# Latent attention of a hybrid encoder: full-precision products of scores and values turned into three rounded products each

## The chip, the cores and the metric

One core of a Trainium2 chip runs the whole program. The metric is the device time of one execution in microseconds (us), the median over several executions. The engines are TensorE (PE in the profile; its weight loads are PEld), VectorE (DVE), ScalarE (ACT), GpSimd (POOL) and SyncE (SP, which issues most transfers).

## What is computed

The reference is one encoder layer over 1024 tokens of width 1024: a layer norm, one input projection, three groups of heads side by side (RWKV-7 time mixing, 2-D neighbourhood attention, latent attention), an output projection, a norm, a SwiGLU FFN and a norm. The change concerns the third group only:

```python
def mla_attention(p, q_norm_g, w_q_b, kv_norm_g, w_kv_b, cos, sin):
    B, T, _ = p.shape
    c_q, c_kv, k_pe = jnp.split(p, [MLA_Q_RANK, MLA_Q_RANK + MLA_KV_RANK], -1)
    q = (rms_norm(c_q, q_norm_g) @ w_q_b).reshape(B, T, MLA_HEADS, MLA_NOPE_DIM + MLA_ROPE_DIM)
    kv = (rms_norm(c_kv, kv_norm_g) @ w_kv_b).reshape(B, T, MLA_HEADS, MLA_NOPE_DIM + MLA_V_DIM)
    q_nope, q_pe = jnp.split(q, [MLA_NOPE_DIM], -1)
    k_nope, v = jnp.split(kv, [MLA_NOPE_DIM], -1)
    q_pe = apply_rope(q_pe, cos[:, None, :], sin[:, None, :])
    k_pe = apply_rope(k_pe, cos, sin)
    q = jnp.concatenate([q_nope, q_pe], -1)
...
    scale = (MLA_NOPE_DIM + MLA_ROPE_DIM) ** -0.5
...
        s = jnp.einsum('bqhd,bkhd->bhqk', q_blk, k).astype(jnp.float32) * scale
        prob = jax.nn.softmax(s, axis=-1)
        return jnp.einsum('bhqk,bkhd->bqhd', prob.astype(v.dtype), v)
```

There are 8 such heads; queries and keys have 64 + 32 columns each, values 64. `k` is `k_nope` with the one `k_pe` beside it in every head. All data are float32.

## The kernel before

Each engine has its own program, written out by hand in the order in which it runs, and the programs meet only through semaphores (`wait_ge`, `then_inc`). Nothing reorders them, so an instruction that waits holds up all that stands behind it on its engine. On-chip memory is one large tile, `arena`, cut by hand into regions; most names in the profile are therefore `arena`. PSUM has eight banks of 512 columns.

The latent attention stands between the neighbourhood attention and the RWKV scan. Its heads are numbered (i, b): pair i from 0 to 3, and b 0 or 1, which also picks the buffers. Eight heads run one after another, and inside a head `kt` counts eight steps of 128 keys. On TensorE a step is:

- `scores` (L1609): keys of the step against all 1024 queries, in two halves of 512 columns, into banks 0 and 1 or 2 and 3 in turn. Rows 0 to 63 hold the plain part, 64 to 95 the rotary part, row 96 of the keys is 1 and row 96 of the queries is minus the row's maximum, so that the maximum is subtracted in the product.
- `values` (L1619): 64 columns of values and 64 columns of ones against the exponentials of the step, summed over the steps in banks 6 and 7. Rows 0 to 63 become the output, rows 64 to 127 the sums of the exponentials.
- `guard` (L1591): rounded scores of the next head, 128 queries against all keys, in banks 4 and 5. VectorE takes their maximum (`head_max`, L1152), which is the maximum that the next head will subtract. The guards were already in the rounded form (`q_round`, `k_round`, type fp32r).

`scores` and `values` take float32 operands; each such product of 512 columns is two matmul instructions in the profile. A rounded product (fp32r) is one.

Between steps ScalarE takes the exponential of a step's scores out of PSUM (`head_exps`, L827) into a ring of three buffers. At the end of a head TensorE turns the maxima into a row (`turn_max`, L1597), which goes by ScalarE (`copy_max`, L798) and a transfer on the SP queue (`head_loads`, L491) into row 96 of the queries; TensorE projects queries, keys and values of the head after next (`head_project`, L1568 and L1572; `head_values`, L1578), ScalarE copies them out (`head_copies`, L784 to L794) and VectorE applies the rotary turn (`head_rope`, L1126 to L1131) and copies the output out (`head_out`, L1158).

Three more things share these engines here. In pair 0, VectorE makes two running sums in each head (`sums`: eight scans L1137, a factor L1139, a sum L1141), and ScalarE makes exponentials of them (`decays`, L808) before steps 2 and 6. While it does so, GpSimd multiplies tiles of 128 x 1024 for the scan (L609 to L620: six instructions for each of four q; the last two wait for `decays`). In pairs 1 to 3, VectorE divides the outputs of the pair before in four pieces (`divide`, L1167 and L1170) while head b = 0 runs.

## Time and profile before

| | |
|---|---|
| median of 3 runs | 1875.41 us (1871.94 to 1876.02) |
| the profiled execution, own time | 1872.56 us |
| its span, first to last instruction | 1870.7 us |
| busy: PE, DVE, ACT, POOL | 92%, 44%, 29%, 19% of the span |
| mean granted TensorE clock | 0.972 |
| latent attention, from the first scores of head (0,0) to the end of head (3,1) | 409.85 to 727.3 us |

The busy shares are means over stages with different limits; what a stage is worth is read from its own rows. A granted clock of 1.00 is TensorE at 2.4 GHz, 0.50 is 1.2 GHz. The chain that ended last is followed back from the end of the program: what stands in it is what the time is made of.

### The profile page before, as it was taken

The numbers are of one execution on the slowest core, as the hardware profiler recorded it, in microseconds if no ns is written. First come the engines' busy times: TensorE is split into PE (matmuls) and PEld (weight loads), VectorE is DVE, ScalarE is ACT, GpSimd is POOL, SyncE is SP. The second block draws the span as 40 slices with busy tenths as digits, with TensorE's granted clock in tenths as the row PEclk, the third lists the DMA queues.
The fourth block names the chain that finished last, engine by engine and source line by source line (L and its number), as shares of the span: only waits on it lengthen the run. The fifth ranks groups of instructions, "written<-read, shape, count | busy, mean of one in ns | idle before, by whom it ended". The sixth has DMA issues, their size and how long they took to land.

```text
span 1870.7 us, 22729 instructions
## 1 busy us (share of the span) xinstructions
PE 1722.4 (92%) x8988; PEld 1224.1 (65%) x8988; DVE 824.8 (44%) x1161; ACT 534.1 (29%) x994; POOL 348.7 (19%) x359
## 2 busy tenths in 40 slices
PE   2999988889999987899999997999999999999995
PEld 2888745644444443577774455888888888888884
DVE  7324329765545444666655365111111111233546
ACT  3111167734333332444441012112111111232321
POOL 0700001128200000877860044000000000000000
PEclk8999999989999998899999998999999999999998
DMA  5311000000000000000005003111111111244233
GB/s 194 117 63 45 12 30 1 1 16 5 4 4 4 4 1 14 2 3 2 2 2 213 12 12 135 46 45 45 54 58 45 45 45 45 81 155 132 93 101 112
DMA packets 24278, 93.50 MB, mean 50 GB/s; under 512 B 2752, under 2 KB 5120, under 8 KB 23568
## 3 DMA queue, kind: packets, MB, share of 16 engines
q1 hardware_dynamic: 23744, 87.27, 13.7%
q0 software_dynamic: 464, 5.28, 0.7%
q8 instruction: 46, 0.75, 0.2%
q14 instruction: 24, 0.20, 0.0%
HBM read 79.92 MB, written 12.58 MB: 49 GB/s over the span
## 4 chain that ended last, share of the span: by engine, by line
PE 87%; DVE 8%; ACT 3%; issue 1%; DMA 1%; SPq 0%; POOL 0%; DVEq 0%; ACTq 0%; POOLq 0%
PE psum L1860 26%; PE psum L1886 12%; PE psum L1468 9%; PE psum L1609 6%; PE psum L1811 6%; PE psum L1619 5%; PE psum L1486 2%; PE psum L1568 2%; PE psum L1550 2%; PE psum L1591 2%; PE psum L1531 1%; PE psum L1493 1%; PE psum L1710 1%; DVE stats L1152 1%; PE psum L1706 1%
## 5 line engine op out<-in xcount | busy, mean ns | idle before, releaser
L1860 PE MATMUL psum<-h_hi,w_hi 128*128 128x512 f32 x704 | 275.2, 391 | 11.7 <-DVE h_lo L1348 11.7
L1860 PE MATMUL psum<-h_lo,w_hi 128*128 128x512 f32 x704 | 274.6, 390 | 0.0
L1860 PE MATMUL psum<-h_hi,w_lo 128*128 128x512 f32 x704 | 274.6, 390 | 0.0
L1381 DVE TENSOR_TENSOR arena<-psum,arena 128x1024 f32 (+1 forms) x22 | 26.9, 1225 | 391.7 <-ACT arena L928 391.7
L1860 PEld LDWEIGHTS psum<-h_hi,w_hi 128*128 128x128 f32 x704 | 132.7, 188 | 39.9 <-DVE h_lo L1348 12.0
L1860 PEld LDWEIGHTS psum<-h_lo,w_hi 128*128 128x128 f32 x704 | 132.6, 188 | 27.7 <-issue 0.2
L1860 PEld LDWEIGHTS psum<-h_hi,w_lo 128*128 128x128 f32 x704 | 132.6, 188 | 27.6
L1152 DVE TENSOR_REDUCE stats<-psum 128x1 f32<-128x1024 f32 x64 | 78.0, 1224 | 122.8 <-PE psum L1591 122.8
L1886 PE MATMUL psum<-wd_hi,act_hi 128*128 128x512 f32 x336 | 130.7, 389 | 0.0
L1886 PE MATMUL psum<-wd_lo,act_hi 128*128 128x512 f32 x336 | 130.7, 389 | 0.0
L1886 PE MATMUL psum<-wd_hi,act_lo 128*128 128x512 f32 x336 | 130.7, 389 | 0.0
L631 POOL TENSOR_TENSOR arena<-arena,consts 128x512 f32<-128x512 f32 x64 | 80.9, 1285 | 265.4 <-ACT arena L864 264.8
L1609 PE MATMUL psum<-arena 97*128 97x512 f32 x256 | 121.6, 602 | 3.2 <-DMA arena<-arena 2.2
L1619 PE MATMUL psum<-arena 128*128 128x512 f32 x256 | 120.3, 592 | 0.0
L1811 PE MATMUL psum<-arena 128*128 128x512 f32 x256 | 111.0, 593 | 1.9 <-DMA arena<-in_w_out 1.9
L1394 DVE TENSOR_TENSOR wd_lo<-arena,wd_hi 128x1024 fp32r<-128x1024 f32 x44 | 53.9, 1225 | 129.7 <-ACT wd_hi L942 129.7
L1468 PE MATMUL psum<-h_hi,w_in_hi 128*128 128x512 f32 x240 | 95.3, 397 | 11.1 <-DVEq L1013 11.1
L827 ACT ACTIVATE arena<-psum 128x1024 f32<-128x1024 f32 x64 | 65.4, 1022 | 133.5 <-PE psum L1609 133.5
L928 ACT ACTIVATE arena<-psum 128x1024 f32 (+1 forms) x22 | 22.6, 1027 | 273.9 <-PE psum L1860 273.9
L1468 PE MATMUL psum<-h_hi,w_in_lo 128*128 128x512 f32 x240 | 95.2, 397 | 0.0
L1468 PE MATMUL psum<-h_lo,w_in_hi 128*128 128x512 f32 x240 | 94.7, 395 | 0.0
L1811 PEld LDWEIGHTS psum<-arena 128*128 128x128 f32 x256 | 48.3, 190 | 63.7 <-issue 59.3
(263 smaller groups left out, 2851.6 us busy)
## 6 DMA issues: line engine op xcount, KB each, us to landing
arena<-in_w_down SPq DMA_DIRECT2D x44, 512.0 KB, 3.6
arena<-in_w_gate SPq DMA_DIRECT2D x22, 512.0 KB, 3.6
arena<-in_w_up SPq DMA_DIRECT2D x22, 512.0 KB, 4.6
arena<-in_w_in SPq DMA_DIRECT2D x15, 512.0 KB, 3.5
arena<-in_x SPq DMA_DIRECT2D x8, 512.0 KB, 9.7
resid_spill<-arena POOLq DMA_DIRECT2D x1, 4096.0 KB, 12.9
arena<-in_w_out SPq DMA_DIRECT2D x8, 512.0 KB, 6.6
arena<-resid_spill SPq DMA_DIRECT2D x1, 4096.0 KB, 20.0
```

What stands on the lines that cost most here:

```text
L631: pool.tensor_tensor(Lev[d][m % 2], Araw[i % 2][d], four_heads(cst((C_LV if d == 0 else C_LVT) + m - 1)), ALU.mult).then_inc(lev_ready, 1)
L827: act.activation(halves(e_ring[(kt) % NE]), psum[:, 2 * (kt % 2):2 * (kt % 2) + 2, :], ACT.Exp, scale=MLA_SCALE).then_inc(e_ready, 1)
L1152: v.tensor_reduce(g_max[:, b, t:t + 1], psum[:, g_banks, :], AX.XY, ALU.max, negate=True).then_inc(g_max_ready, 1)
L1394: v.tensor_tensor(wd_lo[b], raw_w[b], wd_hi[b], ALU.subtract).then_inc(wd_lo_ready, 1)
L1468: mm = pe.matmul(bank(2 * b + hf), w[:, P * k:P * k + P], x[k][:, cols], start=(k == 0 and n == 0), stop=(k == KT - 1 and n == 2))
L1486: mm = pe.matmul(bank(t), x[k][:, t * P:(t + 1) * P], wv_parts[k // 2][:, HALF * (k % 2):HALF * (k % 2) + HALF], start=(k == 0 and n == 0) ...
L1550: mm = pe.matmul(bank(4 + b, P), na_et[:, b, j * P:(j + 1) * P], vals[:, first // 2 + j, hp * P:(hp + 1) * P], start=(j == 0), stop=(j == 3))
L1609: mm = pe.matmul(bank(2 * (kt % 2) + hf), kT[b][0:97, kt * P:(kt + 1) * P], qT[b][0:97, hf * HALF:(hf + 1) * HALF], start=True, stop=True)
L1619: mm = pe.matmul(bank(6 + hf), vh[b][:, kt, :], e_ring[kt % NE][:, hf * HALF:(hf + 1) * HALF], start=(kt == 0), stop=(kt == NT - 1))
L1811: mm = pe.matmul(bank(mixed_bank(t) + hf), mix[:, k, t * P:(t + 1) * P], w_out[k][:, hf * HALF:(hf + 1) * HALF], start=(k == 2), stop=(k = ...
L1860: mm = pe.matmul(bank(4 * b + 2 * n + hf), w[b][n][:, P * k:P * k + P], x[k][:, cols], start=(k == 0 and i == 0), stop=(k == KT - 1 and i ...
L1886: mm = pe.matmul(bank(2 * t + hf), x[b][:, t * P:(t + 1) * P], w[b][:, hf * HALF:(hf + 1) * HALF], start=(free is not None and i == 0), st ...
```

## The change

Queries, keys, values and exponentials are each kept as two rounded tiles, a high part and what is left (`q_hi` and `q_lo`, and so on), and each product of `scores` and `values` becomes three rounded ones: high by high, high by low, low by high. The high parts are written by ScalarE, the low parts are a subtraction on VectorE. The exponential of a step is taken twice from PSUM, once in float32 and once rounded. The values of a step are multiplied two steps behind its scores, not one; the ring of exponentials has two buffers for three. The projection of queries moves ahead of the last values of a head. The row of maxima is now also copied by ScalarE, which waits for the transfer. The guards read the high parts.

```diff
@@ ScalarE
+            def copy_queries(i, b):
                 act.wait_ge(pr_q, 2 * i + (b + 1))
+                act.activation(halves(q_hi[b][0:64, :]), psum[0:64, 0:2, :], ACT.Copy).then_inc(q_nope, 1)
...
             def copy_max(i, b):
                 act.wait_ge(mt_done, 2 * i + (b + 1))
                 act.activation(max_row[0:NT, b, :], psum[0:NT, 4, 0:P], ACT.Copy).then_inc(mt_copied, 1)
+                act.wait_ge(max_in[b], 16 * i + 16)
+                act.activation(q_hi[b][96:97, :], q_raw[b][96:97, :], ACT.Copy).then_inc(max_ready, 1)
...
                     act.wait_ge(s_done, 16 * i + (8 * b + kt + 1))
                     if kt >= NE:
                         act.wait_ge(pv_done, 16 * i + (8 * b + kt - NE + 1))
-                    act.activation(halves(e_ring[(kt) % NE]), psum[:, 2 * (kt % 2):2 * (kt % 2) + 2, :], ACT.Exp,
-                                   scale=MLA_SCALE).then_inc(e_ready, 1)
+                    scored = psum[:, 2 * (kt % 2):2 * (kt % 2) + 2, :]
+                    act.activation(halves(e_ring[kt % NE]), scored, ACT.Exp, scale=MLA_SCALE)
+                    if kt >= 2:
+                        act.wait_ge(pv_done, 16 * i + (8 * b + kt - 1))
+                    act.activation(halves(e_hi[kt % 2]), scored, ACT.Exp, scale=MLA_SCALE).then_inc(e_ready, 1)
@@ VectorE
+            for b in range(2):
+                v.tensor_copy(k_hi[b][64:96, :], k_raw[64:96, :]).then_inc(kpe_ready, 1)
+            v.wait_ge(kpe_ready, 5)
+            for b in (1, 0):
+                v.tensor_tensor(k_lo[b][64:96, :], k_raw[64:96, :], k_hi[b][64:96, :], ALU.subtract).then_inc(kpe_ready, 1)
...
+            def head_parts(i, b, before=False):
                 v.wait_ge(pr_q, 2 * i + (b + 1))
...
+                v.tensor_tensor(turned, psum[64:96, 0:2, :], turned, ALU.add).then_inc(q_rope, 1)
+                v.wait_ge(q_nope, 2 * i + (b + 1))
+                v.tensor_tensor(halves(q_lo[b][0:64, :]), psum[0:64, 0:2, :], halves(q_hi[b][0:64, :]),
+                                ALU.subtract).then_inc(q_split, 1)
+                v.wait_ge(k_nope, 2 * i + (b + 1))
+                v.tensor_tensor(halves(k_lo[b][0:64, :]), psum[0:64, 2:4, :], halves(k_hi[b][0:64, :]),
+                                ALU.subtract).then_inc(k_split, 1)
+                if before:
+                    head_out(i - 1, b)
+                v.wait_ge(v_ready, 2 * i + (b + 1))
+                v.tensor_tensor(vl[b], psum[:, 4:6, :].rearrange("p h (t c) -> p (h t) c", c=P)[:, :, 64:128],
+                                vh[b][:, :, 0:64], ALU.subtract).then_inc(v_split, 1)
+                v.wait_ge(q_rounded, 2 * i + (b + 1))
+                v.tensor_tensor(q_lo[b][64:96, :], q_raw[b][64:96, :], q_hi[b][64:96, :], ALU.subtract).then_inc(q_split, 1)
...
+            def split_exp(i, b, kt):
+                v.wait_ge(e_ready, 16 * i + (8 * b + kt + 1))
+                v.tensor_tensor(e_lo[kt % NE], e_ring[kt % NE], e_hi[kt % 2], ALU.subtract).then_inc(e_split, 1)
+
+            def head_steps(i, b, ahead, beside):
+                nxt = (i + (b + 1) // 2, (b + 1) % 2)
+                for kt in range(NT):
+                    if ahead and kt:
+                        row_max(*nxt, kt - 1)
+                    if ahead and kt == NT - 1:
+                        row_max(*nxt, kt)
+                    split_exp(i, b, kt)
+                    beside(kt)
@@ TensorE
-                for hf in range(NH):
-                    mm = pe.matmul(bank(2 * (kt % 2) + hf), kT[b][0:97, kt * P:(kt + 1) * P],
-                                   qT[b][0:97, hf * HALF:(hf + 1) * HALF], start=True, stop=True)
+                for n, (k_part, q_part, rows) in enumerate(((k_hi, q_hi, 97), (k_hi, q_lo, 96), (k_lo, q_hi, 96))):
+                    for hf in range(NH):
+                        mm = pe.matmul(bank(2 * (kt % 2) + hf), k_part[b][0:rows, keys_at],
+                                       q_part[b][0:rows, hf * HALF:(hf + 1) * HALF], start=(n == 0), stop=(n == 2))
...
+                for n, (part, e_part) in enumerate(((0, e_hi[kt % 2]), (1, e_hi[kt % 2]), (0, e_lo[kt % NE]))):
+                    if n == 2:
+                        pe.wait_ge(e_split, 16 * i + (8 * b + kt + 1))
+                    for hf in range(NH):
+                        mm = pe.matmul(bank(6 + hf, rows=slice(0, 64 if part else P)), (vl if part else vh)[b][:, kt, :],
+                                       e_part[:, hf * HALF:(hf + 1) * HALF], ...
...
                 for kt in range(NT):
                     scores(i, b, kt, ahead)
+                    if ahead and kt == NT - 1:
+                        guard(*nxt, kt - 1)
+                    if kt >= 2:
+                        values(i, b, kt - 2)
+                    if ahead and kt:
+                        guard(*nxt, kt if kt == NT - 1 else kt - 1)
+                values(i, b, NT - 2)
                 if ahead:
                     turn_max(*nxt)
                 if ahead2:
-                    head_project(i + 1, b)
+                    project_q(i + 1, b)
+                values(i, b, NT - 1)
+                if ahead2:
+                    project_k(i + 1, b)
                     pe.wait_ge(mt_copied, 2 * nxt[0] + (nxt[1] + 1))
                     head_values(i + 1, b)
```

Before the first head, the guards of head (0,0) now wait for `kpe_ready` at 7 and for `v_split`, where they waited for ScalarE's rounded copies.

Where the order shows it best is VectorE in head (0,0). Before, eight maxima (L1152) and two groups of running sums stood there; of those, this is the half from the second group on, with the output copy and the rotary turn behind it:

```order
L1137 SCALAR_TENSOR_TENSOR arena<-consts,arena 128x128 x8
L1139 TENSOR_SCALAR stats<-arena 128x8
L1141 TENSOR_TENSOR arena<-arena,stats 128x1024
L1152 TENSOR_REDUCE stats<-psum 128x1 x4
L1158 COPY arena<-psum 64x1024
L1126 TENSOR_TENSOR arena<-psum,arena 32x1024
L1128 TENSOR_TENSOR arena<-psum,arena 32x1024
L1131 TENSOR_TENSOR arena<-arena 32x1024
```

After the change the same place, from the split of step 1 to that of step 4, reads (L1180 is `split_exp`, L1164 to L1168 are `sums`, L1174 is `row_max`):

```order
L1180 TENSOR_TENSOR e_lo_86<-arena,e_hi_88 128x1024
L1164 SCALAR_TENSOR_TENSOR arena<-consts,arena 128x128 x8
L1166 TENSOR_SCALAR stats<-arena 128x8
L1168 TENSOR_TENSOR arena<-arena,stats 128x1024
L1174 TENSOR_REDUCE stats<-psum 128x1
L1180 TENSOR_TENSOR e_lo_85<-arena,e_hi_87 128x1024
L1174 TENSOR_REDUCE stats<-psum 128x1
L1180 TENSOR_TENSOR e_lo_86<-arena,e_hi_88 128x1024
L1174 TENSOR_REDUCE stats<-psum 128x1
L1180 TENSOR_TENSOR e_lo_85<-arena,e_hi_87 128x1024
```

A split of 128 x 1024 has come between any two maxima, and the running sums stand between the split of step 1 and the maximum that guard 2 waits for. At the end of the head eight instructions stand where four did:

```order
L1141 TENSOR_TENSOR arena<-psum,arena 32x1024
L1143 TENSOR_TENSOR psum<-psum,arena 32x1024
L1145 TENSOR_TENSOR arena<-psum,arena 32x1024
L1147 TENSOR_TENSOR q_lo_77<-psum,q_hi_73 64x1024
L1150 TENSOR_TENSOR k_lo_79<-psum,k_hi_75 64x1024
L1196 COPY arena<-psum 64x1024
L1155 TENSOR_TENSOR v_lo_83<-psum,v_hi_81 128x512
L1158 TENSOR_TENSOR q_lo_77<-arena,q_hi_73 32x1024
```

The output copy has moved from the head of this group to the sixth place. TensorE's step 3 of head (0,0), from its scores to the next guard, reads after the change (L1663 scores, L1677 values, L1642 guard):

```order
L1663 MATMUL psum<-q_hi_73,k_hi_75 128x512 x2
L1663 MATMUL psum<-q_lo_77,k_hi_75 128x512 x2
L1663 MATMUL psum<-q_hi_73,k_lo_79 128x512 x2
L1677 MATMUL psum<-e_hi_88,v_hi_81 128x512 x2
L1677 MATMUL psum<-e_hi_88,v_lo_83 64x512 x2
L1677 MATMUL psum<-e_lo_86,v_hi_81 128x512 x2
L1640 REGISTER_ALU
L1642 MATMUL psum<-k_hi_76,q_hi_74 128x512 x2
```

The values there are those of step 1, and only their last two matmuls need VectorE's split.

## Rows read from the trace of the kernel before

**Rows 1.** Busy time by stretch: us, then busy us (x instructions) of PE, PEld, DVE, ACT, POOL, then granted clock, DMA share, GB/s.
```profile
409.85:451.90 42.05, 39.42 (x109) 18.78 (x110) 26.46 (x33) 18.47 (x24) 37.65 (x16) 1.00 0.02 5
451.90:493.60 41.70, 39.32 (x110) 18.71 (x110) 24.27 (x32) 18.26 (x24) 18.02 (x8) 1.00 0.02 5
493.60:536.70 43.10, 40.61 (x109) 19.50 (x109) 22.93 (x20) 13.79 (x15) 0.00 (x0) 0.96 0.02 5
536.70:577.20 40.50, 39.05 (x110) 18.82 (x109) 14.68 (x12) 14.02 (x16) 0.00 (x0) 1.00 0.02 5
...
661.20:697.60 36.40, 31.82 (x82) 15.08 (x82) 19.27 (x17) 10.82 (x12) 0.00 (x0) 0.96 0.00 1
697.60:727.30 29.70, 29.61 (x64) 12.78 (x64) 0.05 (x1) 8.23 (x9) 0.00 (x0) 0.94 0.00 0
409.85:727.30 317.45, 299.76 (x799) 142.04 (x799) 145.27 (x146) 111.60 (x127) 55.66 (x24) 0.98 0.01 3
```

**Rows 2.** Chain that ended last, 566 to 622 us: start, us, what.
```profile
569.81 3.44 PE psum L1568 x8
573.24 1.86 PE psum L1572 x4
575.11 1.98 PE psum L1578 x16
...
602.67 1.72 PE psum L1609 x4
604.39 1.72 PE psum L1619 x4
606.11 0.48 PE psum L1591 x2
...
611.53 5.22 PE psum L1568 x8
```

**Rows 3.** Same view, in the FFN, where all products are rounded.
```profile
1199.91 10.20 PE psum L1860 x45
```

**Rows 4.** Costliest groups: shapes xcount | busy us, mean ns | idle before.
```profile
L1394 DVE TENSOR_TENSOR wd_lo<-arena,wd_hi 128x1024 fp32r<-128x1024 f32 x44 | 53.9, 1225 | 129.7 <-ACT wd_hi L942 129.7
```

**Rows 5.** Groups by line, 400 to 770 us.
```profile
L1152 DVE TENSOR_REDUCE stats<-psum 128x1 f32<-128x1024 f32 x56 | 68.5, 1224 | 119.6 <-PE psum L1591 119.5
L827 ACT ACTIVATE arena<-psum 128x1024 f32<-128x1024 f32 x64 | 65.4, 1022 | 133.5 <-PE psum L1609 133.5
...
L1167 DVE RECIPROCAL arena<-arena 128x256 f32<-128x256 f32 x12 | 20.9, 1745 | 0.1
...
L1170 DVE TENSOR_TENSOR arena<-arena 128x256 f32 (+1 forms) x12 | 5.1, 425 | 1.4 <-DVE arena L1167 0.5
```

**Rows 6.** Timeline, first running sums: start, us, engine, line, what [idle before <- releaser].
```profile
428.63 3.80 DVE L1137 TENSOR_TENSOR_SCAN arena<-consts,arena 128x128 f32<-128x128 f32 x8
...
433.41 1.22 DVE L1141 TENSOR_TENSOR arena<-arena,stats 128x1024 f32<-128x1024 f32 x1
...
434.89 2.13 ACT L808 ACTIVATE arena<-arena 128x1024 f32<-128x1024 f32 x2
435.83 0.74 PE L1591 MATMUL psum<-k_round,q_round 96*128 96x512 f32 x2 [1.04 <-DVE stats L1152]
```

**Rows 7.** Timeline, VectorE, before the FFN.
```profile
1089.03 2.83 DVE L1348 TENSOR_TENSOR h_lo<-arena,h_hi 128x512 fp32r<-128x512 f32 x1
```

**Rows 8.** Timeline, GpSimd, same stretch.
```profile
1088.63 2.67 POOL L671 TENSOR_TENSOR arena<-arena 128x1024 f32<-128x1024 f32 x1
```

**Rows 9.** Line L1348 (low parts for the FFN): its instructions, ns min/median/max.
```profile
L1348 DVE TENSOR_TENSOR h_lo<-arena,h_hi x16: 679/1402/2830, 1082.8 to 1138.2; 128x512 fp32r<-128x512 f32 x16
```

**Rows 10.** Timeline before the first guards.
```profile
385.90 1.22 DVE L1131 TENSOR_TENSOR arena<-arena 32x1024 f32<-32x1024 f32 x1
...
389.07 1.15 PE L1591 MATMUL psum<-k_round,q_round 96*128 96x512 f32 x4 [3.61 <-ACT q_round L794]
```

**Rows 11.** Chain that ended last, from head (3,0) to (3,1).
```profile
695.74 1.82 DMA arena<-arena
```

More of the change, by code:

```diff
@@ L582, in _ @@
             pool.wait_ge(vproj_done, NT)
-            pool.memset(q_diag[:, :, :], 0.0).then_inc(qd_zero, 1)
-            pool.wait_ge(qd_zero, 1)
+            own.add(pool.memset(q_diag[:, :, :], 0.0))
+            own.wait()
             pool.wait_ge(evac_a, NM + NSLOT)
@@ L835, in head_exps @@
                                ACT.Copy).then_inc(sums_copied, 1)
-                if ahead and not last:
-                    copy_max(i + (b + 1) // 2, (b + 1) % 2)
                 if ahead2:
-                    head_copies(i + 1, b)
+                    copy_keys(i + 1, b)
             act.sem_inc(sums_copied, 1)
-            head_copies(0, 0)
+            copy_queries(0, 0)
+            copy_keys(0, 0)
             copy_max(0, 0)
-            head_copies(0, 1)
+            copy_queries(0, 1)
+            copy_keys(0, 1)
             for b in range(2):
@@ L1063, in _ @@
             own.wait()
-            v.tensor_tensor(flat, flat, fill, ALU.add).then_inc(bias_ready, 1)
-            v.wait_ge(bias_ready, 1)
+            own.add(v.tensor_tensor(flat, flat, fill, ALU.add))
+            own.wait()
             for j, n in enumerate((2, 1)):
@@ L1174, in pair, with beside @@
                 for b in range(2):
-                    head_max(i + (b + 1) // 2, (b + 1) % 2,
-                             (2 * b, 2 * b + 1) if before is None else None if b else before)
-                    head_out(i, b)
-                    head_rope(i + 1, b)
+                    def beside(kt):
+                        if before is None and kt % 4 == 1:
+                            sums(2 * b + kt // 4)
+                        if before is not None and b == 0 and kt % 2:
+                            divide(before, kt // 2)
+                    head_steps(i, b, True, beside)
+                    head_parts(i + 1, b, True)
             v.sem_inc(o_ready, 1)
             v.sem_inc(normed, 4)
-            head_rope(0, 0)
-            head_max(0, 0, pairs=2)
-            head_rope(0, 1)
+            head_parts(0, 0)
+            for t in range(NT):
+                row_max(0, 0, t, pairs=2)
+            head_parts(0, 1)
             pair(0, None)
@@ L1189, in _, with beside_last @@
                 own.leave(HEADS // 2 - 2)
-            head_max(HEADS // 2 - 1, 1, HEADS // 2 - 2)
-            for b in range(2):
-                head_out(HEADS // 2 - 1, b)
+            def beside_last(kt):
+                if kt % 2:
+                    divide(HEADS // 2 - 2, kt // 2)
+            head_steps(HEADS // 2 - 1, 0, True, beside_last)
+            head_out(HEADS // 2 - 1, 0)
+            head_steps(HEADS // 2 - 1, 1, False, lambda kt: None)
+            head_out(HEADS // 2 - 1, 1)
             v.wait_ge(sums_copied, HEADS + 1)
@@ L1590, in guard @@
                 for hf in range(NH):
[L1591 to L1592 removed]
+                    mm = pe.matmul(bank(4 + 2 * (t % pairs) + hf), q_hi[b][0:96, t * P:(t + 1) * P],
+                                   k_hi[b][0:96, hf * HALF:(hf + 1) * HALF], start=True, stop=True)
                 mm.then_inc(g_done, 1)
```

142 lines of the change are left out of this document (66 added, 76 removed).

## The prediction

> **What bounds the kernel now.** I read the busy time by stretch first. The latent attention lasts 317.45 us, and TensorE is busy for 299.76 of them; VectorE has 145.27, ScalarE 111.60, GpSimd 55.66 [rows 1]. The chain that ended last says the same: one step is 1.72 us of scores, 1.72 of values and 0.48 of guard, and nothing stands between them [rows 2]. So TensorE sets the pace and the others have slack, but not the same slack in each head. In the heads of pair 0 VectorE is busy for 26.46 and 24.27 of 42 us, since it makes the running sums there, and in heads (1,0), (2,0) and (3,0), which divide, for about 23 of 43; in (1,1) for 14.68 of 40.5 [rows 1]. Where it has most to do it already shows: after the first sums a guard waits 1.04 us for a maximum [rows 6], and the projections behind (2,0) take 5.22 us in place of 3.44 [rows 2], since TensorE had stopped for the divide and its granted clock fell (0.96 over that kind of head against 1.00, [rows 1]). The question is whether VectorE can carry what the change gives it.
>
> **TensorE, what is removed.** In the FFN a rounded product of 512 columns takes 10.20 / 45 = 0.227 us [rows 3]; the guard's pair takes 0.47 to 0.48 [rows 2]. I take 0.2325 us each. Six for a step's scores are 1.40 us against 1.72, and the same for the values. A step falls from 3.91 to 2 x 1.40 + 0.47 = 3.26 us. Over 64 steps that is 128 x 0.32 = 41 us of TensorE, were nothing else in the way. A head's floor becomes 8 x 3.26 + 3.44 + 1.86 + 1.98 for the projections [rows 2] + 0.3 for the turn = 33.7 us. (The Trainium skill, FP8 and Floating Point Precision, TensorE Precision Notes, gives true FP32 four passes through the array. By it three passes for four would save a quarter of 1.72, 0.43 a product and 55 us in all; the rows say 0.32, and they go into the sum.) One doubt: the product with the low values has 64 output rows, and the only product here of that shape, L1572, takes 1.86 / 4 = 0.465 where L1568 takes 0.43. From below, no cost; from above, 2 x 0.035 us in 64 steps, 4.5 us. I take none, since both of those are full-precision products.
>
> **ScalarE.** A step has two exponentials of 1.02 us [rows 5] where it had one: 2.04 of 3.26 us. With three copies of 1 us, one of 0.6, the sums' copy and the new copy of the maxima it comes to some 23 us in a head of 34 or more. It doesn't bind by its load. It does lengthen chains: a step's exponentials now end 2.0 us after their start, not 1.0.
>
> **VectorE, what is added.** Each step gets a subtraction of 128 x 1024, 1.225 us by the same instruction in the FFN [rows 4], beside the maximum of 1.224 [rows 5]: 8 x 2.45 = 19.6 us a head. The head's end has eight instructions: seven at about 1.22 and the low values, 128 x 512, at half, 0.65; 9.2 us. With 0.03 between instructions VectorE has 29.3 us in every head. To that come 4 x (1.745 + 0.425) = 8.7 us, with their own waits 9.0, in a head that divides [rows 5], and in pair 0 two groups of sums, each 433.41 + 1.22 - 428.63 = 6.0 us [rows 6]. So VectorE has 29.3 us in (1,1) and (2,1), 38.3 in (1,0) and (2,0), 41.3 in (0,0) and (0,1), against 33.7 of TensorE. It becomes the bound in four heads, and what TensorE saves there is not seen.
>
> **Head by head.**
> (1,1), (2,1): TensorE binds. Exposed: guard 0 waits for the low values, scores 2 for two exponentials, some maxima come late by 0.1 to 0.2; I give 1.5 us in all. 35.2 against 40.5 [rows 1]: -10.7 for both.
> (1,0), (2,0): VectorE binds, 38.3, and while TensorE projects queries (3.44 us, behind the last maximum) it has one split and one divide to fill the time, then waits; 1.3 us. 39.6 against 43.1: -7.0 for both. (Pair 2 takes 317.45 less the six stretches shown, 84.0 us, against 83.6 of pair 1.)
> (3,0): VectorE's 8 steps and the divide, 28.9 us, then the turn, the row (ScalarE 0.3, transfer 1.82 [rows 11], the new copy 1.0): about 33 against 36.40. (3,1): no guards, 8 x 2.8 + 1.3 for the last split and 2 for a low clock at its start (0.94 over that head now [rows 1]): 25.8 against 29.70. Both: -7.3.
> Before the first scores: the guards of (0,0) began at 389.07, released by ScalarE's rounded copy, 1.95 us after VectorE's rotary turn had ended (387.12) [rows 10]. Now VectorE must do a copy (0.7), two low parts of the keys (2.45), the low queries and keys (2.45) and values (0.65) first: 6.3 less 1.95, +4.3 us.
>
> **Pair 0.** Three things beyond the 41.3 us of load. First, VectorE stands idle behind ScalarE. Exponential 2 stands behind `decays`, which need the sums. From the end of the sums it is 2.4 us of decays [rows 6] and 2.0 of two exponentials to the split of step 2, and VectorE has only one maximum of 1.2 to do: 3.3 us idle, twice a head. With 2.6 us at the head's end (3.44 + 0.4 for the projected queries less the split of 1.22) a head takes 41.3 + 6.6 + 2.6 = 50.5 us. Two are 101.0 against 83.75: +17.3.
>
> Second, GpSimd. At 1089.03 a subtraction of VectorE with both inputs in `arena`, 128 x 512, took 2.83 us [rows 7]; its shortest takes 0.679 [rows 9]. A GpSimd product was running from 1088.63 to 1091.30 [rows 8], and VectorE ended 0.56 us behind that end: it was held until the GpSimd instruction was over. The splits of exponentials have both inputs in `arena` too, and during pair 0 GpSimd runs 24 instructions in 55.66 us, 2.3 us each [rows 1]. Over some 105 us it is running half of the time, so 17 such instructions wait 17 x 0.53 x 1.15 = 10 us, all on VectorE, the bound. From below nothing, if they fall in gaps; from above, each is held for most of one instruction, 20 us. I take 10. (The Trainium skill, GPSIMD Engine Reference, Key points, says that GpSimd shares its SBUF interfaces with VectorE and contends with instructions that have two SBUF inputs. The trace agrees; by the rule the low queries, keys and values, which read PSUM, would not be held.)
>
> Third, the clock. TensorE will stop for 3 us and more six times in pair 0. A stop cost 5.22 - 3.44 = 1.8 us behind (2,0) [rows 2]. From below nothing, where VectorE is late anyway; from above 11. I take 5. Pair 0: 17.3 + 10 + 5 = +32.3 us, 116 in place of 83.75.
>
> **Sum.** 4.3 + 32.3 - 10.7 - 7.0 - 7.3 = +11.6 us. On the profiled execution's own 1872.56 that is 1884.2; the median of the runs shown lies 2.85 above it, so I forecast 1886 us. Nothing behind 727.3 changes: the RWKV scan and the FFN keep their instructions.
>
> **Rivals.**
> *Pair 0 costs only its load and its idle times.* If the splits mostly fall where GpSimd waits for `decays`, and the stops cost nothing more, the sum is 4.3 + 17.3 - 25.0 = -3.4: 1872. It decides at a hold of about 4 us for all splits together. For it: GpSimd waits for ScalarE in pair 0 (18.02 busy of 41.70 [rows 1]). Against it: [rows 7, 9]. With part of the hold the result is within 0.2%. Together 0.22.
> *TensorE binds everywhere.* If VectorE ran its new work beside the old at no cost to the guards, all seven heads with guards would gain 5.2 and the last 5.2: -41 + 4.3, 1839 us. It would need VectorE to finish 41.3 us in 34 in pair 0; chance 0.03.
> *The low clock spreads.* If small stops in the heads bound by VectorE leave TensorE at half clock for long, a step there takes twice 3.26 = 6.5 us. A quarter of the steps of six heads so, 12 x 3.2 = 39 us at most, half of it hidden by VectorE: 1886 + 17 = 1903. Against it: pair 0 kept a clock of 1.00 in spite of stops of 1 us [rows 1, 6]. With a hold of 20 us it gives the same time. Chance 0.17.
> The forecast has 0.58.
>
> **Range and chances.** A measurement of this kernel tells about 0.2%, 3.75 us. The range goes from 1869 (first rival, 3 us better in the heads bound by TensorE) to 1904. Faster: 0.03 and half of the first rival's 0.22, 0.14. Same, the other half of it, 0.11. Slower: the forecast and the last rival, 0.75.
>
> **What would show it.** In the profile after: L1663 and L1677 at about 0.23 us a product in the chain; stretches of 50 to 60 us for heads (0,0) and (0,1), about 39 or 40 for (1,0), about 35 for (1,1); VectorE above 95% busy in (1,0); waits of guards for the maximum (L1174) after each sums, 3 to 7 us long; splits (L1180) of 2 to 3.5 us beside GpSimd's products in pair 0 and of 1.22 later. I am wrong if pair 0 lasts under 105 us, or if splits never exceed 1.3 us.

## The result and the profile after

The changed kernel takes 1879.08 us (median of 20 runs, 1875.81 to 1883.75); the kernel before, run beside it 20 times too, 1874.59 us. The ratio is 1.0026 [1.0018, 1.0033]: slower by 4.5 to 4.9 us. The spans of the two profiled executions are 1876.3 and 1870.7 us. The changed kernel's trace is 2.05 us behind already where the projections for head (0,0) begin (379.96 against 377.91 us), ahead of the whole stage; over the traces of this document that moment varies from 377.8 to 382.2 us. So times ahead of the first scores are counted from there.

The page after, busy time by engine. TensorE falls from 92% to 90%, VectorE rises from 44% to 50%:

```profile
PE 1697.1 (90%) x9244; PEld 1268.6 (68%) x9244; DVE 942.0 (50%) x1260; ACT 593.1 (32%) x1057; POOL 358.7 (19%) x359
```

Busy time by stretch, which answers to [rows 1]: heads (0,0) to (3,1), then all of the latent attention (columns: stretch, its length, busy us and instructions of PE, PEld, DVE, ACT, POOL, clock, DMA share, GB/s):

```profile
416.89:475.40 58.51, 41.84 (x142) 27.27 (x142) 44.77 (x44) 24.56 (x30) 42.84 (x16) 0.80 0.02 4
475.40:530.00 54.60, 41.45 (x144) 27.34 (x142) 40.99 (x45) 25.73 (x31) 22.26 (x8) 0.81 0.02 4
530.00:568.00 38.00, 35.29 (x144) 23.43 (x142) 35.84 (x33) 21.44 (x23) 0.00 (x0) 1.00 0.02 6
568.00:603.20 35.20, 34.41 (x143) 23.58 (x141) 28.11 (x25) 21.44 (x23) 0.00 (x0) 1.00 0.02 6
603.20:641.20 38.00, 35.28 (x143) 23.45 (x141) 35.84 (x33) 21.45 (x23) 0.00 (x0) 1.00 0.02 5
641.20:676.40 35.20, 34.41 (x143) 23.59 (x141) 28.12 (x25) 21.44 (x23) 0.00 (x0) 1.00 0.00 0
676.40:708.70 32.30, 28.18 (x115) 19.45 (x113) 31.22 (x29) 18.38 (x20) 0.00 (x0) 1.00 0.00 1
708.70:734.20 25.50, 24.56 (x96) 18.07 (x96) 10.71 (x10) 16.60 (x19) 0.00 (x0) 0.93 0.00 0
416.89:734.20 317.31, 275.42 (x1055) 186.19 (x1055) 255.59 (x237) 171.03 (x191) 65.10 (x24) 0.92 0.01 4
```

The last row is the point: 317.31 us, where it was 317.45 [rows 1]. TensorE has 24 us less to do and VectorE 110 us more, and the stage lasts as long as before. Six heads got faster by 4.1 to 5.4 us each, together 29.5, and the two heads of pair 0 gave 29.4 back: 58.5 and 54.6 where they took 42.05 and 41.70, at a granted clock of 0.80 in place of 1.00. The loss that is left lies ahead of the first scores. TensorE's timeline there, which answers to [rows 10]:

```profile
395.35 2.05 PE L1642 MATMUL psum<-k_hi,q_hi 96*128 96x512 f32 x4 [7.84 <-DVE v_lo L1155]
...
416.89 0.73 PE L1663 MATMUL psum<-q_hi,k_hi 97*128 97x512 f32 x2 [1.25 <-DVE q_lo L1147]
```

The guards waited 3.61 us for ScalarE; now they wait 7.84 us for VectorE's low values, and the first scores wait another 1.25 us for the low queries. From the first projections to the first scores it is 36.93 us, where it was 31.94.

What pair 0 looks like, in the chain that ended last (start us, us, what):

```profile
420.55 2.62 DVE e_lo L1180
423.16 1.14 DVE stats L1174
424.30 1.13 DVE e_lo L1180
425.43 5.47 DVE arena L1164 x8
...
431.13 1.23 DVE arena L1168
...
434.64 1.01 ACT arena L832
435.65 0.92 ACT e_hi L835
...
436.61 2.93 PE psum L1663 x6
439.54 1.80 PE psum L1677 x6
441.34 0.47 PE psum L1642 x2
441.81 1.39 PE psum L1663 x6
```

Read it downwards. VectorE carries the chain for 12 us: a split held to 2.62 us, then the eight scans, 5.47 us where the group in [rows 6] took 3.80. ScalarE's decays and two exponentials follow, and only then can TensorE make the next scores. But for one guard it has been idle since 427.9, 5.68 and then 1.85 us, and the six products take 2.93 us; the same six take 1.39 us five microseconds later. That is TensorE at 1.2 and then at 2.4 GHz. VectorE's own timeline shows its side of the same stop:

```profile
436.59 1.72 DVE L1180 TENSOR_TENSOR e_lo<-arena,e_hi 128x1024 fp32r<-128x1024 f32 x1 [3.10 <-ACT e_hi L835]
```

So both engines wait for ScalarE: exponential 2 stands behind the decays, and these wait for the sums that VectorE itself has just made.

The place of the sums is part of this. The group in [rows 6] is the second of head (0,0), not the first. The first stood ahead of all maxima in the kernel before, and VectorE's timeline there shows that the first maximum came right behind it, with no wait of TensorE for it:

```profile
409.64 2.63 DVE L1137 TENSOR_TENSOR_SCAN arena<-consts,arena 128x128 f32<-128x128 f32 x8
...
415.76 1.23 DVE L1152 TENSOR_REDUCE stats<-psum 128x1 f32<-128x1024 f32 x1
```

In the changed kernel both groups of a head stand later, behind the splits of steps 1 and 5, right in front of the decays that need them (the decays are where they were). No run changes back this alone.

Over pair 0 the waits (engine, line, what for: us, times, longest) are:

```profile
PE psum L1642 <- DVE stats L1174: 25.7, 7, 6.3
DVE e_lo L1180 <- ACT e_hi L835: 14.8, 9, 3.1
```

The splits of the two halves of the stage, first pair 0, then all heads behind it (ns, shortest/median/longest):

```profile
L1180 DVE TENSOR_TENSOR e_lo<-arena,e_hi x16: 1207/1629/2617, 420.5 to 519.0; 128x1024 fp32r<-128x1024 f32 x16
L1180 DVE TENSOR_TENSOR e_lo<-arena,e_hi x48: 1211/1224/1226, 534.3 to 732.1; 128x1024 fp32r<-128x1024 f32 x48
```

Behind pair 0 GpSimd is silent in this stage and no split exceeds 1.226 us.

### The profile page after: what moved, and what is told of

It reads as the page before. It is cut to its first block, busy times and chain, and to the rows that moved or that the text cites. A ratio compares the mean times of both kernels' runs of the same rounds, so it can differ in the third digit from the quotient of the medians.

```text
span 1876.3 us, 23427 instructions
## 1 busy us (share of the span) xinstructions
PE 1697.1 (90%) x9244; PEld 1268.6 (68%) x9244; DVE 942.0 (50%) x1260; ACT 593.1 (32%) x1057; POOL 358.7 (19%) x359
## 4 chain that ended last, share of the span: by engine, by line
PE 77%; DVE 14%; ACT 4%; issue 3%; DMA 1%; POOL 1%; SPq 0%; DVEq 0%; ACTq 0%; POOLq 0%
PE psum L1926 26%; PE psum L1952 12%; PE psum L1516 9%; PE psum L1877 6%; PE psum L1677 2%; PE psum L1663 2%; DVE e_lo L1180 2%; PE psum L1534 2%; PE psum L1598 2%; DVE stats L1174 2%; PE psum L1616 1%; PE psum L1579 1%; PE psum L1541 1%; DVE arena L1164 1%; PE psum L1776 1%
## 5 line engine op out<-in xcount | busy, mean ns | idle before, releaser
L1877 PE MATMUL psum<-arena 128*128 128x512 f32 x256 | 111.0, 593 | 1.2 <-DMA arena<-in_w_out 1.1
L937 ACT ACTIVATE arena<-psum 128x1024 f32 (+1 forms) x22 | 22.6, 1027 | 273.9 <-PE psum L1926 273.9
L1516 PE MATMUL psum<-h_hi,w_in_hi 128*128 128x512 f32 x240 | 94.5, 394 | 11.1 <-DVEq L1022 11.1
L1180 DVE TENSOR_TENSOR e_lo<-arena,e_hi 128x1024 fp32r<-128x1024 f32 x64 | 84.7, 1324 | 32.3 <-ACT e_hi L835 32.1
L951 ACT ACTIVATE wd_hi<-arena 128x1024 fp32r<-128x1024 f32 x44 | 46.7, 1060 | 148.4 <-PE psum L1952 148.4
L1642 PE MATMUL psum<-k_hi,q_hi 96*128 96x512 f32 x128 | 50.3, 482 | 43.5 <-DVE stats L1174 34.9
```

The costliest lines, as they stand in the source:

```text
L951: act.activation(wd_hi[b], raw_w[b], ACT.Copy).then_inc(wd_hi_ready, 1)
L1180: v.tensor_tensor(e_lo[kt % NE], e_ring[kt % NE], e_hi[kt % 2], ALU.subtract).then_inc(e_split, 1)
L1516: mm = pe.matmul(bank(2 * b + hf), w[:, P * k:P * k + P], x[k][:, cols], start=(k == 0 and n == 0), stop=(k == KT - 1 and n == 2))
L1642: mm = pe.matmul(bank(4 + 2 * (t % pairs) + hf), q_hi[b][0:96, t * P:(t + 1) * P], k_hi[b][0:96, hf * HALF:(hf + 1) * HALF], start=True, s ...
L1877: mm = pe.matmul(bank(mixed_bank(t) + hf), mix[:, k, t * P:(t + 1) * P], w_out[k][:, hf * HALF:(hf + 1) * HALF], start=(k == 2), stop=(k = ...
```

## The experiments

Times are medians; each ratio is against the kernel before, run beside it. The changed kernel's own ratio is 1.0026, and one thousandth is 1.9 us. First scores to first scores is the length of a head.

**GpSimd's products left out.** The 24 products of pair 0 aren't computed; the scan behind gets unfinished inputs.

```diff
             for q in range(4):
-                own.add(pool.tensor_tensor(Bt[:, q], Kt[:, q], kk[:, hp], ALU.mult))
-                ...
                 pool.wait_ge(ex_ready, 4 * (q + 1))
-                ...
+                pool.sem_inc(kb_ready, 1)
```

> The changed kernel with GpSimd's 24 products of pair 0 left out (their results are not made; one fill of 128 x 4096 stands in their place). In the changed kernel's trace the splits of pair 0 exceed 1.22 us by 6.7 us in all and three groups of eight scans take 5.54 us where one takes 2.62, 8.8 us more: 15.5 us of VectorE being held. Theory A, holds by GpSimd are on the path: splits back to 1.22, scans to 2.6 everywhere, 9 to 13 us faster than the changed kernel, about 1868. Theory B, VectorE idles behind ScalarE's decays anyway and the holds fall into that: under 4 us faster, 1876 or more.

Measured: 1872.27 us, ratio 0.9978 [0.9968, 0.9988], which is 8 to 9 us below the changed kernel, at the lower edge of theory A. Heads (0,0) and (0,1) fall from 58.5 and 54.6 to 51.5 and 51.4. VectorE's costliest groups over pair 0:

```profile
L1172 DVE TENSOR_TENSOR e_lo<-arena,e_hi 128x1024 fp32r<-128x1024 f32 x16 | 19.5, 1221 | 14.8 <-ACT e_hi L827 14.8
...
L1156 DVE TENSOR_TENSOR_SCAN arena<-consts,arena 128x128 f32<-128x128 f32 x32 | 10.5, 400 | 0.0
```

The same groups of the changed kernel:

```profile
L1180 DVE TENSOR_TENSOR e_lo<-arena,e_hi 128x1024 fp32r<-128x1024 f32 x16 | 26.2, 1637 | 14.8 <-ACT e_hi L835 14.8
...
L1164 DVE TENSOR_TENSOR_SCAN arena<-consts,arena 128x128 f32<-128x128 f32 x32 | 19.2, 670 | 0.0
```

So GpSimd costs VectorE 6.7 us in the splits, where the prediction had 10, and 8.7 us in the scans, which I had not counted. Of these 15.4 us some 10 reach the end of pair 0. The idle time behind the exponentials is 14.8 us in both. The same edit on the kernel before is the control:

> The kernel before with GpSimd's 24 products of pair 0 left out (same edit as in the first experiment; their results are not made). Control: leaving them out bought 8.5 us in the changed kernel. Theory A, the change made VectorE's held instructions matter: here only the scans and one factor are held, and TensorE waits 1.04 us for it, so 0 to 3 us faster. Rival: GpSimd costs both kernels alike (for instance by SBUF traffic), 6 us or more faster here too.

Measured: 1873.43 us, ratio 0.9992 [0.9982, 1.0002]. GpSimd holds up VectorE there as well (the second group of scans takes 3.80 us where an unheld one takes 2.63), but VectorE has more slack: pair 0 gets 2.7 us shorter in the trace, against 10.3 in the changed kernel.

**Decays two steps later.** ScalarE takes the decays before steps 4 and 7, not 2 and 6.

```diff
-                    if with_decays and kt in (2, 6):
-                        decays(2 * b + kt // 4)
+                    if with_decays and kt in (4, 7):
+                        decays(2 * b + (kt == 7))
```

> The changed kernel with ScalarE's decays moved from before steps 2 and 6 to before steps 4 and 7 of the heads of pair 0; the sums stay where they are. Theory C, the exponentials of step 2 and 6 standing behind decays that wait for the sums is what makes VectorE idle for 3.1 us and TensorE wait 1.85 us after each guard: the four idle times go, pair 0 falls from 113.1 to about 97 to 100 us, about 14 us faster in all (1865), which is faster than the kernel before. Rival D, VectorE's load alone (41 us a head) is the bound and the idle time is only moved: under 4 us faster.

Measured: 1869.46 us, ratio 0.9967 [0.9952, 0.9982], 11 us below the changed kernel by the ratios, 8.7 by the spans. Heads (0,0) and (0,1) take 53.2 and 48.5, 101.7 in all, a little short of theory C's 97 to 100. The stop behind the decays was real. But the scans still hold up the maxima (the guards wait 22.6 us in all, where they waited 25.7) and the clock stays at 0.81 and 0.86.

**Values one step behind the scores.** All else as changed.

```diff
                 for kt in range(NT):
                     scores(i, b, kt, ahead)
+                    if kt:
+                        values(i, b, kt - 1)
+                    if ahead and kt:
+                        guard(*nxt, kt - 1)
                     if ahead and kt == NT - 1:
-                        guard(*nxt, kt - 1)
-                    if kt >= 2:
-                        values(i, b, kt - 2)
-                    if ahead and kt:
-                        guard(*nxt, kt if kt == NT - 1 else kt - 1)
-                values(i, b, NT - 2)
+                        guard(*nxt, kt)
```

> The changed kernel with the values one step behind the scores again, as in the kernel before; all else as changed. Theory E, the second step behind is needed since values now stand behind two exponentials and a subtraction: the wait comes back in every step, 4 to 5 us a head, 20 to 35 us slower than the changed kernel, about 1907. Rival F, TensorE has scores and a guard (1.87 us) and the previous values (1.4 us) to cover 2.2 us of exponentials and 1.3 of subtraction, so only the low product waits: at most 5 us slower.

Measured: 1926.66 us, ratio 1.0268 [1.0248, 1.0289]: dearer than I expected, 46 us over the changed kernel. From one step's first scores to the next's it is 3.66 us (596.77 to 600.43), where the load of TensorE is 3.26:

```profile
596.77 0.63 PE L1663 MATMUL psum<-q_hi,k_hi 97*128 97x512 f32 x2
...
599.38 0.74 PE L1677 MATMUL psum<-e_lo,v_hi 128*128 128x512 f32 x2
599.96 0.63 PE L1642 MATMUL psum<-k_hi,q_hi 96*128 96x512 f32 x2
600.43 0.63 PE L1663 MATMUL psum<-q_hi,k_hi 97*128 97x512 f32 x2
```

Two exponentials and a split don't fit behind one step of TensorE. Heads (1,0) and (1,1) take 46.5 and 42.3. At 0.40 us a step that is some 3 of the 7.1 us that (1,1) loses; the rest lies at the head's end, where this edit also puts two guards back to back, and in the clock, 0.93 and 0.96 there. Both heads are slower than in the kernel before (43.1 and 40.5). No run has the one step of distance without the two guards in a row.

**One half of the change each.** First the scores alone as three products; values and exponentials as before, still two steps behind. There are no splits of exponentials and values and no second exponential.

```diff
-                    act.activation(halves(e_ring[kt % NE]), scored, ACT.Exp, scale=MLA_SCALE)
...
-                    act.activation(halves(e_hi[kt % 2]), scored, ACT.Exp, scale=MLA_SCALE).then_inc(e_ready, 1)
+                    act.activation(halves(e_ring[kt % NE]), scored, ACT.Exp, scale=MLA_SCALE).then_inc(e_ready, 1)
...
-                    split_exp(i, b, kt)
```

> Half of the change: scores as three rounded products of split queries and keys, values in float32 as before (one exponential a step, no subtraction of exponentials, no low values), values still two steps behind with a ring of three. Theory A/C, VectorE's splits of exponentials are what loses: VectorE has 9.8 us less a head, TensorE's step is 1.40 + 1.72 + 0.47 = 3.59 us; heads (1,0) to (2,1) 37.5 to 38.5 us, pair 0 about 80 us, in all some 12 to 18 us faster than the kernel before, about 1860. Rival G, the longer head end (low queries and keys, copied maxima) costs what the scores save: within 4 us of the kernel before.

Measured: 1855.93 us, ratio 0.9897 [0.9878, 0.9916]. By stretch, heads (0,0) to (1,1):

```profile
414.27:463.25 48.98, 41.10 (x126) 23.77 (x126) 30.62 (x35) 17.22 (x22) 35.91 (x16) 0.90 0.02 5
463.25:507.49 44.24, 38.39 (x129) 22.26 (x127) 28.92 (x36) 18.40 (x23) 18.54 (x8) 0.96 0.02 5
507.49:543.70 36.21, 36.21 (x128) 21.73 (x127) 26.66 (x24) 14.23 (x15) 0.00 (x0) 1.00 0.02 6
543.70:579.91 36.21, 36.21 (x128) 21.73 (x127) 18.17 (x16) 14.22 (x15) 0.00 (x0) 1.00 0.02 6
```

Behind pair 0 TensorE isn't idle for a moment, and a head takes 36.2 us: one more than (1,1) of the full change, 1.8 less than (1,0), and less than the 37.5 to 38.5 expected. Pair 0 was expected at about 80 us and takes 93.2. The two misses go opposite ways, and that the time came out near the expected one is in part luck. Even here pair 0 is 9.5 us slower than before; the guards wait 11.4 us for maxima in it. A step has less TensorE work to cover the sums, the sums stand later, and the low queries and keys have come to VectorE: no run separates these.

Then the values alone: scores in full precision with rounded copies for the guards, as before, and no low queries and keys.

```diff
-                for n, (k_part, q_part, rows) in enumerate(((k_hi, q_hi, 97), (k_hi, q_lo, 96), (k_lo, q_hi, 96))):
-                    for hf in range(NH):
-                        mm = pe.matmul(bank(2 * (kt % 2) + hf), k_part[b][0:rows, keys_at],
-                                       q_part[b][0:rows, hf * HALF:(hf + 1) * HALF], start=(n == 0), stop=(n == 2))
+                for hf in range(NH):
+                    mm = pe.matmul(bank(2 * (kt % 2) + hf), kT[b][0:97, keys_at],
+                                   qT[b][0:97, hf * HALF:(hf + 1) * HALF], start=True, stop=True)
```

> The other half of the change: values and exponentials split, values as three rounded products, two steps behind; scores in full precision, with rounded copies for the guards, as before. A step of TensorE is 1.72 + 1.40 + 0.48 = 3.60 us, VectorE has the splits of the exponentials but not the low queries and keys. Theory A (what costs in pair 0 is the splits of exponentials beside the sums): pair 0 lasts 100 to 106 us, heads (1,0) and (1,1) 36.4 to 37, and the first guards begin as early as before; the sum is near the kernel before or up to 8 us below it, 1867 to 1874. Theory B (the low parts at the head's end cost as much as the splits do): pair 0 falls to about 92 us and the time to 1858.

Measured: 1879.02 us, ratio 1.0020 [1.0009, 1.0031]. Both theories miss: pair 0 lasts 111.3 us, not 100 to 106 or 92, head (1,0) 38.1, and the time is above 1874. Head (1,1) with 36.8 us is as expected, and so are the first guards, 11.1 us behind the first projections here and 11.2 in the kernel before.

```profile
412.04:469.40 57.36, 43.59 (x125) 24.11 (x126) 40.64 (x41) 25.16 (x31) 40.37 (x16) 0.85 0.01 4
469.40:523.37 53.97, 43.31 (x127) 23.68 (x126) 35.74 (x41) 25.44 (x32) 20.79 (x8) 0.87 0.02 4
523.37:561.49 38.12, 37.02 (x128) 20.62 (x126) 32.46 (x29) 21.18 (x24) 0.00 (x0) 1.00 0.02 5
561.49:598.31 36.82, 36.36 (x128) 20.70 (x126) 24.83 (x21) 21.17 (x24) 0.00 (x0) 1.00 0.02 6
```

VectorE is busy for 9 us less over pair 0 than in the full change, and pair 0 is only 2 us shorter; but TensorE's step is 0.34 us longer here, so this alone doesn't settle what binds. The changed kernel's own rows do: VectorE is busy for 85.8 of the 113.1 us of pair 0 and idle for 27.4, most of it behind ScalarE's exponentials (14.8) and TensorE's projections (8.7). Its load is not the bound; a chain from engine to engine is.

Scores alone lengthen pair 0 by 9.5 us, values alone by 27.6, both by 29.4. These are not parts of one sum, since each half also holds what both have in common: the later place of the sums and the two steps between scores and values. What the full change has over scores alone (the second exponential, the split of each step, the low values) costs 19.9 us in pair 0; which of them costs it, no run shows.

**No division.** Reciprocal and product are left out of heads (1,0), (2,0) and (3,0), so the outputs stay undivided.

```diff
-                own.add(v.reciprocal(inv_sum[:, cols], inv_sum[:, cols]))
-                own.wait()
-                out = mix[:, ds(4 + i, 1), cols].rearrange("p o c -> p (o c)")
-                v.tensor_tensor(out, out, inv_sum[:, cols], ALU.mult).then_inc(normed, 1)
+                v.sem_inc(normed, 1)
```

> The changed kernel with the division of the outputs (reciprocal and product, 4 x 2.2 us in heads (1,0), (2,0) and (3,0)) left out, so that the outputs stay undivided. Theory A (VectorE binds the heads that divide): heads (1,0) and (2,0) fall from 38.0 us to the 35.2 of (1,1), (3,0) from 32.3 to about 31.5; the time is some 6 us below the changed kernel's, 1873 us, level with the kernel before. Theory B (those heads are held by the chain of exponentials and by the new order at the head's end, not by VectorE's load): they stay at 38.0 and the time at 1879.

Measured: 1873.97 us, ratio 0.9990 [0.9979, 1.0001], 5 to 7 us below the changed kernel. Theory A holds; head (3,0) falls further than expected, to 30.0 us. By stretch, heads (1,0) and (1,1):

```profile
529.60:565.01 35.41, 34.70 (x144) 23.61 (x142) 28.30 (x25) 21.45 (x23) 0.00 (x0) 1.00 0.02 6
565.01:600.24 35.23, 34.45 (x143) 23.61 (x141) 28.12 (x25) 21.45 (x23) 0.00 (x0) 1.00 0.02 6
```

**Sums spread out.** One group of sums in each of the heads (0,0), (0,1), (1,1) and (2,1), which don't divide, and in small pieces: two scans at each of steps 0 to 3, the rest at step 4, the decays before exponential 6. The loops over pairs 1 and 2 are written out for it. Nothing is left out.

```diff
+        SUMS_IN = ((0, 0), (0, 1), (1, 1), (2, 1))
...
-                        if before is None and kt % 4 == 1:
-                            sums(2 * b + kt // 4)
+                        if (i, b) in SUMS_IN and kt < 4:
+                            scans(SUMS_IN.index((i, b)), (2 * kt, 2 * kt + 1))
+                        if (i, b) in SUMS_IN and kt == 4:
+                            sums(SUMS_IN.index((i, b)))
...
-                    if with_decays and kt in (2, 6):
-                        decays(2 * b + kt // 4)
+                    if (i, b) in SUMS_IN and kt == 6:
+                        decays(SUMS_IN.index((i, b)))
```

On the kernel before:

> The kernel before with the running sums spread: one q in each of the heads (0,0), (0,1), (1,1) and (2,1), two scans a step over steps 0 to 3, factor and sum at step 4, decays before step 6. Control for the next two. Where sums stood TensorE waited some 1 us a group, four groups: 2 to 5 us faster than the kernel before (1871 to 1873). More than 8 us would say that the burst of sums already cost the kernel before what it costs the changed one.

Measured: 1879.07 us, ratio 1.0022 [1.0012, 1.0033]. A miss: slower, not faster. Its heads take 41.4, 41.5, 43.3, 41.5, 43.3, 41.1 and 36.4 us, so pair 0 gains 0.8 and (1,1) and (2,1) lose 1.6 together; (3,1), with no sums of its own, loses another 1.4. From the first projections to the end of (3,1) its trace is 2 us longer than that of the kernel before; where the other 2 us lie I did not find. It isn't the longer programs. This is shown by the kernel before with the loops written out and nothing else:

> The kernel before with the loops over pairs 1 and 2 written out on ScalarE and VectorE, as the kernels with spread sums have them, and nothing else. If the 4 us that the spread sums cost the kernel before came from the longer programs, this one is 3 to 4 us slower than it, ratio 1.002; if they came from the sums in heads (1,1) and (2,1), this one is level, 0.999 to 1.001.

Measured: 1875.27 us, ratio 0.9997 [0.9988, 1.0006].

On the changed kernel:

> The whole change, with the running sums spread in the same way. Theory C, what loses is the burst of 6 to 9 us of sums between a split and a maximum, with the decays behind it and the low clock after it, and not the load of VectorE as such: heads (0,0) and (0,1) fall from 58.5 and 54.6 to 40 to 43 us, (1,1) and (2,1) stay within 2 us of 35.2: about 25 to 28 us faster than the changed kernel, 1852 to 1856. Rival D, the load is the bound and holds by GpSimd spread with it: 10 us or less faster than the changed kernel.

Measured: 1852.49 us, ratio 0.9875 [0.9859, 0.9891], 28 us below the changed kernel and within the expected range. The granted clock is 1.00 from (0,0) to (2,1) and pair 0 lasts 77.8 us in place of 113.1; (0,1) with 37.2 us is below the 40 to 43 expected, and (1,1) and (2,1) pay 2.0 us each:

```profile
420.21:460.79 40.58, 35.43 (x141) 23.36 (x142) 36.32 (x34) 22.45 (x26) 27.07 (x10) 1.00 0.02 6
460.79:498.00 37.21, 34.73 (x143) 23.53 (x141) 33.26 (x35) 23.65 (x27) 15.11 (x6) 1.00 0.02 6
498.00:535.68 37.68, 35.18 (x143) 23.43 (x141) 35.88 (x33) 21.45 (x23) 0.00 (x0) 1.00 0.02 6
535.68:572.91 37.23, 34.73 (x144) 23.53 (x142) 33.28 (x35) 23.65 (x27) 15.12 (x6) 1.00 0.02 5
```

The edit does several things at once. It cuts the sums into pieces, takes two of the four groups out of pair 0, lets the first decays wait until exponential 6, and with the decays it moves a part of GpSimd's products to later heads (42 us of them are left in pair 0, of 65). Alone were tried only the later decays (11 us) and no products at all (8 to 9). How much is due to the pieces and how much to the other heads is open, and so is what the old place of the sums would have given.

**Sums spread out, and scores alone.** The scores-only kernel with this spread.

> Scores alone split (values in float32 as before), with the running sums spread. In scores-only, pair 0 took 49.0 and 44.2 us and every later head 36.2 without any stop of TensorE. Theory C: pair 0 falls to 37 to 38 us a head, 17 to 19 us faster than scores-only, 1837 to 1840; it then beats the whole change with spread sums by 10 us or more. Rival: TensorE's lower floor in the whole change (33.7 against 36.2 us a head) wins once the sums are spread, and the whole change is the faster of the two.

Measured: 1836.62 us, ratio 0.9796 [0.9783, 0.9810]: 38 us below the kernel before, the best of all here and 16 below the whole change with spread sums. Its profiled execution is the slowest of its five (1843.90 us), but the stage in it is the shortest of all here. Two of its heads, then the whole stage; TensorE is busy 271.86 of 273.96 us:

```profile
418.54:455.59 37.05, 36.51 (x125) 21.67 (x126) 25.94 (x25) 15.36 (x18) 22.55 (x10) 1.00 0.02 6
455.59:491.80 36.21, 36.21 (x128) 21.73 (x127) 22.06 (x26) 16.55 (x19) 13.35 (x6) 1.00 0.02 6
...
418.54:692.50 273.96, 271.86 (x927) 163.28 (x927) 168.24 (x165) 113.80 (x126) 54.00 (x24) 1.00 0.01 4
```

The whole change with spread sums takes 285.55 us for the same stage: 37.2 to 37.7 us a head from (0,1) to (2,1) where this one takes 36.2, and 40.58 in (0,0) where this one takes 37.05. So the values' half of the change costs more than it saves even then. It paid only in heads (1,1) and (2,1) of the changed kernel, where VectorE makes neither sums nor a division: 35.2 us there, 36.2 here.

## Why the prediction was right or wrong

The direction was right and the size was not: +11.6 us forecast, +4.5 to +4.9 measured. The measured terms add up to +4.9. By its own steps:

- **TensorE.** Right. Six products take 1.39 and 1.40 us against the 1.40 forecast, and a step is 3.26. The doubt about 64 output rows is settled by the values (L1677): their six, two of them of that shape, take 1.40 too. No cost, as taken.
- **Heads (1,1) and (2,1), bound by TensorE.** Right: 35.2 us each, -10.6 in all.
- **Heads (1,0) and (2,0), bound by VectorE.** The mechanism is right (without the division they fall to 35.4), the size is not: 38.0 and not 39.6, so -10.5 in place of -7.0. The step that failed is "with 0.03 between instructions VectorE has 29.3 us in every head". I charged 1.25 us for each instruction. The timeline gives each 1.21 to 1.23, but in head (1,0) 17 of the next ones start only 1.13 to 1.16 us later: when nothing is waited for, the rows overlap by 0.08 us. At 0.11 us less than charged, that is 1.9 us, and the head came out 1.6 shorter. The division (some 2.25 us a piece, as charged) and the idle time (0.82 + 0.49 against 1.3) came as forecast.
- **Last pair.** 32.3 and 25.5 against 33 and 25.8: -8.4 in place of -7.3, in (3,0) by the same term.
- **Ahead of the first scores.** +5.0 in place of +4.3. The guards came 4.2 us late; the 1.25 us wait of the first scores for the low queries was missing from the sum.
- **Pair 0.** 113.1 us where I had 116, +29.4 in place of +32.3. The total is near, but its parts are not, and that they cancel is luck:
  - VectorE's own work was charged at 82.6 us (twice 41.3). Without GpSimd's products it is busy for 70.3. Of the difference 4.4 us are the 1.25 us again. The other 7.9 are the sums: I took 6.0 us for every group from [rows 6], but that group was itself held up by GpSimd (scans 3.80 us, the factor 0.92); an unheld one takes 4.0. The hold was thus in the sum twice.
  - The hold by GpSimd is 6.7 us for the splits against 10, but 8.7 more in the scans, 15.4 in all. Leaving GpSimd out gives back 10 us of the trace and 8 to 9 of the time.
  - VectorE's idle time and the clock were put at 18.4 + 5 us; it is idle for 27.4. Behind the decays it waits 3.10 us at a time, as forecast (3.3). The excess lies with the clock and at the heads' ends, where it waits 8.7 us for the projections against 5.2. I gave 5 us for six stops of 3 us and more; there are eight between the steps, of 1.84 to 6.30 us, three of them over 3 us, and the granted clock is 0.80 over both heads. In the chain, the pieces of TensorE that ran slow are 1.9 us too long behind the stop in the middle of a head and 2.8 at its end. That gives an estimate of at most 9.5 us for the pair; 5.6 of them lie where VectorE waits for TensorE.
  - In all: 92.6 busy and 23.4 idle forecast, 85.8 and 27.4 measured.

The error of 6.7 us is thus -2.9 in pair 0, -3.5 in the two heads that divide, -1.1 in the last pair, +0.7 at the start and +0.1 in (1,1) and (2,1). The term that failed everywhere is VectorE's 1.25 us an instruction where most take 1.14. It alone accounts for the 3.5 us in the heads that divide and for 4.4 in pair 0, where the scans, the clock and the doubled hold hide it.

The first rival, pair 0 at only its load and idle times, fell for this kernel, but it describes the one without GpSimd's products: it gave 101 us for the pair and 1872 us, and that kernel has 102.8 and 1872.27. The agreement is in part luck: the rival has VectorE busy for 82.6 us and idle for 18.4, the trace 70.3 and 32.5. The low clock stayed inside pair 0 and the head at the end, and did not spread. That TensorE binds in all heads came true only with the sums in another place and the scores alone. Of the signs named, the splits (up to 2.62 us) and the waits of guards (2.6 to 6.3 us behind each group of sums) came; VectorE is busy for 94% of (1,0), not over 95%.

## What to carry to other kernels

When a change makes the bounding engine faster, look at the stretches in which another engine has extra work to do: what it saves elsewhere can be lost there whole, and moving that extra work (28 us here, at no cost in instructions) can be worth more than the change itself. It has to be measured with the change: on the kernel before, the same move cost 4 us. A step whose result goes from engine to engine (TensorE, ScalarE twice, VectorE) is to be costed as a chain. Look at what stands between its links in each engine's queue, such as eight scans in a row just ahead of the instruction that needs them, and try it in pieces or elsewhere. Try the halves of a change apart: here the scores alone gave the gain, and the values' half lost more than it saved.

## What the runs showed of the hardware

- VectorE's instructions of 1.22 us start 1.13 to 1.14 us apart when nothing is waited for (423.16, 424.30 and 425.43 in the chain). A sum of durations over-charges VectorE by 7% where this is so. Of the instructions of the rotary turn, each of which waits for the one before, the starts are 1.25 to 1.28 us apart. The Trainium skill, Perfetto Trace Analysis, DVE / Act Engine Instruction, says that the shown end is that at which the last written bytes are acknowledged, while the next instruction may begin to read before. This trace agrees.
- GpSimd's hold reaches further than the forecast had it. Three of the four groups of eight scans of 128 x 128 take 5.54 us, beside its instructions; the fourth, in head (0,1), has none beside it and takes 2.62, as all four do with the products left out. In the kernel with scores alone a factor of 128 x 8 (L1160) took 2.15 us and ended when the product beside it did, 425.57 against 425.54; in the changed kernel it takes 0.17:

```profile
423.20 2.34 POOL L620 TENSOR_TENSOR arena<-arena 128x1024 f32<-128x1024 f32 x1
423.42 2.15 DVE L1160 TENSOR_SCALAR stats<-arena 128x8 f32<-128x8 f32 x1
```

- The maxima, which read PSUM, aren't held: one at 463.23 in the changed kernel took 1.23 us inside a product of GpSimd that ran from 462.96 to 465.32.
- TensorE's clock: with stops of 1.85, 2.20, 5.68 and 6.30 us between the steps of head (0,0), the granted clock is 0.80 over that head, and the first six products behind one ran at 1.2 GHz (2.93 us, then 1.39 at 2.4 GHz). Behind a stop of 2.60 us in head (0,1) the guard's pair took 1.22 us, where it takes 0.63 at the full clock. The same two heads with the sums spread out, where the longest stop is 2.07 us, have 1.00.
